# Output projection by seven block products instead of eight block multiplications, w_out split beside the last two branches

## The reference, cut to what matters

```
proj   = x @ W_in                              # 1024 x 9224, columns shared among the branches
y_i    = branch_i(proj) @ P_i                  # four branches A, B, C, M
merged = sum_i sigmoid(g_i) * y_i
out    = merged @ W_out                        # 1024 x 1024 times 1024 x 1024
x      = LayerNorm(alpha * x + out) * ln_g + ln_b
```

## Time and profile before

| | us |
|---|---|
| median of 3 runs | 1212.56 (1212.28 to 1212.91) |
| the profiled execution, whole | 1211.9 |
| its span in the profile | 1210.1 |
| mean granted clock of TensorE | 0.999 of full |
| TensorE busy | 1199.3 (99%) |
| DVE busy | 790.7 (65%) |
| POOL busy | 710.7 (59%) |
| ScalarE busy | 544.6 (45%) |
| output projection, first to last matmul | 1116.2 to 1203.6 |

### The profile page before, as it was taken

One profiled execution on the slowest core, in us unless ns is written; L12 is line 12 of the kernel. 1 busy time (PEld: TensorE's weight loads), 2 busy tenths in 40 slices (PEclk: granted clock), 3 DMA queues, 4 the chain that ended last, 5 costly groups with the idle time before them and its releaser, 6 DMA issues.

```text
span 1210.1 us, 15914 instructions
## 1 busy us (share of the span) xinstructions
PE 1199.3 (99%) x5772; PEld 1003.7 (83%) x5772; DVE 790.7 (65%) x1288; ACT 544.6 (45%) x997; POOL 710.7 (59%) x555
## 2 busy tenths in 40 slices
PE   9999999999999999999999999999999999999997
PEld 7888888888888888888888888888888888888886
DVE  5623865677576674428897666666667686877855
ACT  5433424344443444547474565656556444315000
POOL 6777887887777777878446445455533225558000
PEclk9999999999999999999999999999999999999999
DMA  8012131242323323233512111111002533377231
GB/s 280 15 55 70 35 105 35 70 140 101 108 105 105 131 92 126 105 106 118 196 48 60 36 53 53 36 53 52 20 18 101 187 115 113 105 250 253 79 123 69
DMA packets 91277, 118.61 MB, mean 98 GB/s; under 512 B 6072, under 2 KB 72632, under 8 KB 91200
## 3 DMA queue, kind: packets, MB, share of 16 engines
q1 hardware_dynamic: 90912, 117.34, 29.4%
q10 hardware_dynamic: 288, 0.26, 0.1%
HBM read 92.39 MB, written 25.20 MB: 97 GB/s over the span
## 4 chain that ended last, share of the span: by engine, by line
PE 91%; DVE 5%; ACT 2%; issue 1%; POOL 1%; DVEq 0%; ACTq 0%
PE pj L770 11%; PE pj L772 11%; PE pj L771 11%; PE pj L846 5%; PE pj L847 5%; PE pj L848 5%; PE pj L1119 4%; PE pt L770 3%; PE pt L772 3%; PE pt L771 3%; PE po L960 3%; PE pj L863 2%; PE pj L864 2%; PE pj L865 2%; PE pt L1119 2%; PE po L1119 2%
## 5 line engine op out<-in xcount | busy, mean ns | idle before, releaser
L1634 POOL TENSOR_TENSOR ring_lo<-w_pair,ring_hi 128x512 fp32r<-128x512 f32 x168 | 232.8, 1388 | 109.8 <-ACT ring_hi L1177 109.7
L1687 POOL TENSOR_TENSOR w_lo<-w_raw,w_hi 128x128 fp32r<-128x128 f32 (+1 forms) x104 | 113.0, 1105 | 131.4 <-ACT w_hi L1267 129.3
L1177 ACT ACTIVATE ring_hi<-w_pair 128x512 fp32r<-128x512 f32 x168 | 105.1, 628 | 160.4 <-PE pj L772 108.6
L1856 DVE SCALAR_TENSOR_TENSOR po<-glu,cwa,po 128x512 f32<-128x512 f32 x232 | 159.4, 747 | 20.6 <-ACT po L1228 20.6
L770 PE MATMUL pj<-t_hi,ring_hi 128*128 128x512 f32 x392 | 152.9, 390 | 0.3 <-DVE slot L1820 0.3
L771 PE MATMUL pj<-t_lo,ring_hi 128*128 128x512 f32 x392 | 152.5, 389 | 0.0
L772 PE MATMUL pj<-t_hi,ring_lo 128*128 128x512 f32 x392 | 152.5, 389 | 0.0
L846 PE MATMUL pj<-xT_hi,w_hi 128*128 128x512 f32 x320 | 126.2, 395 | 0.0
L847 PE MATMUL pj<-xT_lo,w_hi 128*128 128x512 f32 x320 | 125.3, 392 | 0.0
L848 PE MATMUL pj<-xT_hi,w_lo 128*128 128x512 f32 x320 | 125.2, 391 | 0.0
L1735 POOL TENSOR_SCALAR probs<-probs,rinv 128x128 f32<-128x128 f32 (+3 forms) x32 | 57.9, 1811 | 108.1 <-DVE rinv L2178 108.1
(11 more groups left out here) (394 smaller groups left out, 3001.9 us busy)
## 6 DMA issues: line engine op xcount, KB each, us to landing
w_pair<-in_w_in SPq DMA_DIRECT2D x28, 1024.0 KB, 5.2
gate_scratch<-slot SPq DMA_DIRECT2D x16, 1024.0 KB, 4.0
gate<-gate_scratch SPq DMA_DIRECT2D x32, 512.0 KB, 3.7
w_raw<-in_w_in SPq DMA_DIRECT2D x20, 512.0 KB, 3.9
z_scratch<-slot SPq DMA_DIRECT2D x8, 512.0 KB, 2.9
bias<-cum_scratch SPq DMA_DIRECT2D x8, 512.0 KB, 3.7
wout_raw<-in_w_out SPq DMA_DIRECT2D x8, 512.0 KB, 6.2
x_tok<-in_x SPq DMA_DIRECT2D x8, 512.0 KB, 4.3
```

The lines of the kernel that those rows point to most:

```text
L1177: nc.scalar.activation(ring_hi[:, j % RING, :, :], w_src(u, p), ACT.Copy).then_inc(s_rhi, 1)
L1634: nc.gpsimd.tensor_tensor(ring_lo[:, j % RING, :, :], w_src(u, p), ring_hi[:, j % RING, :, :], ALU.subtract).then_inc(s_rlo, 1)
L1687: nc.gpsimd.tensor_tensor(w_lo[:, j % 2, k, :], w_raw[:, j % 2, k, :], w_hi[:, j % 2, k, :], ALU.subtract).then_inc(s_wlo, 1)
L1856: nc.vector.scalar_tensor_tensor(out=acc if n < PAD_A else src, in0=src, scalar=cwa[:, ct, n:n + 1], in1=acc, op0=ALU.mult, op1=ALU.add).t ...
```

## The change

The output projection is written like the input projection: 2x2 blocks, seven products. With merged (tokens) in four pairs u of two token tiles and w_out in blocks of 512 x 512 (B11, B12, B21, B22):

- Seven w_out blocks of 512 x 512 take the place of eight rows (`out_block_hi`, `out_block_copy`, `out_block_lo`; the numbers n of `OUT_B`). Three are loaded from w_out itself (n = 0, 3, 5: B11, B21, B22), four are sums of blocks. DVE makes these sums in pairs 3 and 4 of the input projection (`block_sum`, 16 subtractions of 128 x 512, 8 in each pair, ahead of that pair's results), from rows loaded into two buffers, and SP stores them to a DRAM scratch `t_dram`, 1 MB for each row block k. The rows for pair 4 are loaded when pair 3's sums are stored. Two waits on that store are added (ScalarE before the tanh of pair 6, DVE before the sums of the layer norm).
- Pair 4 has 4 convolution steps instead of 8, pair 5 has 12 instead of 8.
- Each block, 1 MB, is loaded behind the gate load at s = M1, M3, M5, C2, C3, C5, C6; at C2 SP first waits until M5 is added up, at C6 until TensorE has finished M7. ScalarE makes the hi part (128 x 2048) and copies the scaled block to PSUM banks 4 to 7 (4 x 512), and DVE subtracts from there.
- From C2 on TensorE uses four banks for the branches and runs four halves ahead, and the last two tiles are done first halves first. DVE adds up the last two tiles itself.
- DVE (u = 0) and POOL (u > 0, and the fourth sum of u = 0) make four sums of merged blocks per u; ScalarE and POOL make hi and lo of the blocks in a ring of five. For u = 0 TensorE waits for the rests of blocks 0 to 5, before its seventh product for those of block 6.
- Results: ScalarE copies products 1, 5 and 6, DVE adds them to alpha * x (`with_copy`), then products 2, 7, 3 are added and 4 directly (`out_result`), each with its statistics. The norm of tile 6 stands before the last result. The last part is 512 columns wide.
- The gates of M2 to M5 move from 16 to 28 KB to 0 to 12 KB, other buffers move too.

```diff
-        count = (8, 8, 8, 8, 8, 8, 6, 6, 16, 16, 14, 14, 16, 16, 14, 14, 16, 16, 14, 14)[u - 4]
+        count = (4, 12, 8, 8, 8, 8, 6, 6, 16, 16, 14, 14, 16, 16, 14, 14, 16, 16, 14, 14)[u - 4]
...
+    OSEQ = [(u, p) for u in range(OU) for p in ORDER]
+    OUT_B = {1: 0, 5: 1, 6: 2, 2: 3, 7: 4, 3: 5, 4: 6}
+    LAST_C = S_END - 2
...
+                if u == 3 or u == 4:
+                    sp.wait_ge(s_ot, 8 * (u - 2))
+                    for k in range(2 * u - 6, 2 * u - 4):
+                        sp.dma_start(t_dram[k, :, :, :], ob_rows[k % 2][:, :, :].rearrange("p a (b c) -> p (a b) c", b=2)
+                                     ).then_inc(s_ots, 16)
+                if u == 2 or u == 3:
+                    if u == 2:
+                        sp.wait_ge(s_grp, 8)
+                        sp.wait_ge(s_xbl, 12)
+                    else:
+                        sp.wait_ge(s_ots, 32)
+                    for k in range(2 * u - 4, 2 * u - 2):
+                        for n in range(2):
+                            sp.dma_start(ob_rows[k % 2][:, n, :], w_out[(k + KH * n) * P:(k + KH * n + 1) * P, :]
+                                         ).then_inc(s_wor, 16)
...
-                if s == S_OF[BR_C, 2]:
+                if s == S_OF[BR_M, 1]:
                     sp.wait_ge(s_tlo, TB_PAIR * CT + 2 * NT)
                     sp.wait_ge(s_pv, PV_PAIR * CT + 2 * NT)
                     sp.wait_ge(s_zpre, CT + MP)
-                    for k in range(2):
-                        sp.dma_start(wout_raw[k][:, :], w_out[k * P:(k + 1) * P, :]).then_inc(s_wo[k], 16)
...
+                    load_out_block(0)
+                if s in (S_OF[BR_M, 3], S_OF[BR_M, 5]):
+                    load_out_block((s - S_OF[BR_M, 1]) // 2)
+                if s == S_OF[BR_C, 2]:
+                    sp.wait_ge(*added(S_OF[BR_M, 5]))
+                    load_out_block(3)
+                if s in (S_OF[BR_C, 3], S_OF[BR_C, 5]):
+                    load_out_block(4 + (s - S_OF[BR_C, 3]) // 2)
+                if s == S_OF[BR_C, 6]:
+                    sp.wait_ge(s_pj, 2 * S_OF[BR_M, DT - 1] + 2)
+                    load_out_block(6)
...
+            for h in range(2):
+                for s in range(LAST_C, S_END):
+                    pe.wait_ge(s_pjfree, half_no(s, h) - 4)
+                    p_steps(s, h, 0, CT, branch_bank(s, h))
...
+                pe.wait_ge(s_orl, j + 1)
+                if u == 0:
+                    pe.wait_ge(s_obl, KH * (7 if p == 4 else 6))
+                dst = out_bank(u, p)
+                for k in range(KH):
+                    w_h, w_l = o_ring_hi[j % O_RING][:, k, :], o_ring_lo[j % O_RING][:, k, :]
+                    hi, lo = ob_hi[OUT_B[p]][:, k, :], ob_lo[OUT_B[p]][:, k, :]
+                    nc.tensor.matmul(dst, w_h, hi, start=k == 0 and p in (1, 2, 5), stop=False, skip_group_check=True)
+                    nc.tensor.matmul(dst, w_h, lo, start=False, stop=False, skip_group_check=True)
+                    mm = nc.tensor.matmul(dst, w_l, hi, start=False, stop=k == KH - 1, skip_group_check=True)
...
+            def block_sum(k, n):
+                b11, b12, b21, b22 = (ob_rows[k % 2][:, q // 2, q % 2 * HALF:(q % 2 + 1) * HALF] for q in range(4))
+                if n == 0:
+                    dve.wait_ge(s_wor, 64 * (k // 2 + 1))
+                else:
+                    dve.wait_ge(s_ot, 4 * k + n)
+                dst, in0, in1 = ((b11, b12, b11), (b12, b22, b12), (b22, b22, b11), (b21, b21, b22))[n]
+                nc.vector.tensor_tensor(dst, in0, in1, ALU.subtract).then_inc(s_ot, 1)
...
+                    if u in (3, 4) and i < 3:
+                        for n in range(3 * i, min(3 * i + 3, 8)):
+                            block_sum(2 * (u - 3) + n // 4, n % 4)
...
+                if s >= S_OF[BR_C, 2] - 1:
+                    out_block_lo(s - S_OF[BR_C, 2] + 1)
+            for h in range(2):
+                for s in range(LAST_C, S_END):
+                    p_half(s, h, branch_bank(s, h))
+                if h == 0:
+                    for n in (1, 3, 2):
+                        merged_sum(dve, nc.vector, 0, n)
+                    out_block_lo(5)
```

More of the change, by code:

```diff
@@ L1094, in _ @@
                     mscores(w + 2)
[L1095 removed]
+            for s in range(S_P + IN_M, LAST_C):
                 for h in range(2):
@@ L1149, in w_src @@
+            for j in range(NOQ):
+                out_product(j)
         def w_src(u, p):
@@ new lines, in out_block_copy @@
+            def out_block_copy(n):
+                for k in range(KH):
+                    if n == 0:
+                        act.wait_ge(s_pjfree, HALF_0 + 16)
+                    elif n < 6:
+                        act.wait_ge(s_obl, KH * (n - 1) + k + 1)
+                    elif k < 2:
+                        act.wait_ge(s_pjfree, 2 * S_END)
+                    else:
+                        act.wait_ge(s_obl, KH * n + k - 1)
+                    nc.scalar.activation(block_bank(n, k), ob_raw[n][:, k, :], ACT.Copy, scale=0.5).then_inc(s_obc, 1)
@@ L1626, in _ @@
                                      bias=eps[:, 0:1]).then_inc(s_osd, 1)
+            for s in range(S_P + IN_M + 2, S_END):
+                split_w(s // 2, s % 2, p_k(s))
+                if s in (S_OF[BR_M, 5], S_OF[BR_M, 7]):
+                    out_block_hi((s - S_OF[BR_M, 5]) // 2)
+                n = s - S_OF[BR_C, 2]
+                if n in (0, 2, 3, 4, 5):
+                    out_block_copy(max(n - 1, 0))
+                if n in (1, 2, 3, 5):
+                    out_block_hi({1: 2, 2: 3, 3: 4, 5: 5}[n])
+            for j in range(O_RING):
+                out_ring_hi(j)
+                if j == 0:
+                    out_block_copy(5)
+            out_block_hi(6)
+            for u in range(OU):
+                for p in ORDER:
+                    if p in (1, 5, 6):
+                        out_copy(u, p)
+                    if u and p == 5:
+                        out_std(2 * u - 1)
+                    if OSLOT[u, p] + O_RING < NOQ:
+                        out_ring_hi(OSLOT[u, p] + O_RING)
+                    if (u, p) == (0, 5):
+                        out_block_copy(6)
+                    if p == 4:
+                        out_std(2 * u)
+            out_std(NT - 1)
         @block.gpsimd
@@ L1778, in _, with out_lo @@
                     add_back(s - 2)
+            def out_lo(j):
+                pool.wait_ge(s_orh, j + 1)
+                nc.gpsimd.tensor_tensor(o_ring_lo[j % O_RING][:, :, :], out_src(*OSEQ[j]), o_ring_hi[j % O_RING][:, :, :],
+                                        ALU.subtract).then_inc(s_orl, 1)
+            for u in range(OU):
+                for p in ORDER:
+                    if p == 1 and u:
+                        merged_sum(pool, nc.gpsimd, u, 1)
+                        merged_sum(pool, nc.gpsimd, u, 3)
+                    out_lo(OSLOT[u, p])
+                    if p == 1 and u:
+                        merged_sum(pool, nc.gpsimd, u, 2)
+                    if p == 2:
+                        merged_sum(pool, nc.gpsimd, u, 4)
         @block.vector
@@ L2416, in _ @@
                                                    in1=lnb_b[:, part], op0=ALU.mult, op1=ALU.add).then_inc(s_yo, 1)
+            for u in range(OU):
+                for p in (1, 5, 6):
+                    if (u, p) == (0, 6):
+                        out_block_lo(6)
+                    with_copy(u, p)
+                for p in (2, 7, 3):
+                    out_result(u, p)
+                out_mean(2 * u)
+                if u < OU - 1:
+                    out_norm(2 * u)
+                    out_result(u, 4)
+                    out_mean(2 * u + 1)
+                    out_norm(2 * u + 1)
+            out_norm(NT - 2)
+            out_result(OU - 1, 4)
+            out_mean(NT - 1)
+            out_norm(NT - 1)
 def kernel(**inputs):
```

327 lines of the change are left out of this document (194 added, 133 removed).

## The result

| | before | after |
|---|---|---|
| median | 1212.49 us (4 runs) | 1227.75 us (4 runs, 1226.31 to 1228.40) |
| profiled execution, whole | 1211.9 | 1228.39 |
| its span | 1210.1 | 1226.6 |
| first matmul of the output projection | 1116.19 | 1138.02 |
| end of its last matmul | 1203.6 | 1217.7 |

The ratio is 1.0125, 95% interval 1.011 to 1.014: the change makes the kernel 15.3 us slower, and 1226 had been forecast. The sum was nearly right, but two of its terms were wrong in opposite directions.

What follows compares the result with a forecast made beforehand. TensorE, busy 99% of the span, was taken as the bound, with each wait put before it. Span 1210.1 - 10.9 + 7.0 + 13.4 + 2.3 + 1.5 = 1223.4; with 2.5 more, 1226 us, range 1211 to 1234.

Steps and rivals of the forecast that it cites:

- TensorE's work: Output projection: 336 matmuls of 512 columns instead of 384, 48 saved at 0.2267 us each, -10.9 us.
- rival D: Output projection: DVE becomes the bound through waits for POOL, 22 us per pair, +9, 1235 us; chance 0.05.
- The block sums beside pair 4: Input projection: late rows and turns with POOL delay DVE's sums and results, so TensorE waits; +7.0 us, bounds 4 and 9.
- Rivals A and C: First: pair 4 not held up, 1218 us, chance 0.12; second: one queue's transfers overlap fully, 1206 us, 0.11.
- The split of w_out: Branches M and C: larger block loads delay weights, gates and the projection's first product; +13.4 us, bounds 2 and 18.
- step (a): Branch M: blocks 1 and 2 queue ahead of weights, landing 3.1 us later each; M5's addition ends 1087.5, not 1083.0.
- rival B: Branches M and C: weights and gates pass the blocks in the queue, delays shrink to 1.5 us, 1213 us; chance 0.12.
- Step (b): Branches M to C: SP waits for M5's addition before block 3, so M7's gate lands 7.6 us later, at 1095.2.
- Step (c): Before the projection: from 1095.2 DVE has 28.4 us of work plus 6 us of late gates; first product at 1129.6.
- Clock: TensorE after two long waits: half clock until it recovers, as long as the fall; +1.5 us, between 0 and 2.9.
- End: After the last matmul: tile 6's norm makes the last result 1.8 us late, its 512 width adds 0.5; +2.3 us.

Runs made afterwards that it cites:

- e1: Changed kernel with the second eight block sums in pair 5 instead of pair 4, convolution steps 8 and 8; 1217.28 us, ratio 1.0042 to the kernel before.
- e6: Changed kernel with no rows loaded for pair 4, whose sums reuse pair 3's rows (other values); 1216.44 us, ratio 1.0036 to the kernel before.
- e7: Changed kernel with w_out blocks 1 and 2 loaded from ScalarE's DMA queue instead of SP's; 1228.30 us, ratio 1.0128 to the kernel before.
- e2: Changed kernel with SP's wait for M5's addition and block 3's load moved behind C3's weights and M7's gate; 1224.74 us, ratio 1.0101 to the kernel before.
- e4: Changed kernel with the projection's first pair in PSUM banks 0, 2, 3, each product awaiting only its own block's rests; 1219.86 us, ratio 1.0062 to before.
- e10: Changed kernel with the edits of e1, e2 and e4, block 1 loaded one tile earlier, and tile 6 stored without its norm; 1207.66 us.
- e9: Changed kernel with the edits of e1 and e4 together; 1210.72 us, ratio 0.9988 to the kernel before.

## Why the prediction was right or wrong

**TensorE's work**, -10.9: right. 336 matmuls at 0.2267 us, with two gaps of 0.24 us among them, apart from those at half clock; rival D (DVE as the bound of the projection) did not come.

**The block sums beside pair 4**, +7.0: right in mechanism and size (7.3). Its steps: rows forecast at 95.5, landed at 97.87; the store took 10.1 us and not 8. The eight sums were to end at 112.0, with two results; it was 112.3, because the turns cost less than the 16.5 us counted (a sum and its turn took about 1.7 us and not 1.9). So two errors of 2 us cancelled, which was luck. The 104.08 of the forecast is the start of DVE's next result; the seventh product itself began at 103.88. That the sums wait for POOL in turns is borne out: six of them take 9.25 us where each alone takes 0.7. Rivals A and C fall with the wait itself; e1 and e6 show its cause.

**The split of w_out**, +13.4: wrong by 3.8 us (9.6 measured), and in its step (a) wrong in mechanism. "A later small load lands behind a block" is true of the trace, but e7 shows that a queue of its own does not free the small load: 7.9 us for M4's weights there, 6.9 in the changed kernel. The forecast had ruled on rival B by that row ("against it: 1086.53"), and the row cannot tell the order of a queue from full engines. For the time here it made no difference; it would have led one to the wrong cure. Step (b) held to a microsecond: M5 added at 1097.50 (forecast 1087.5 + 10.65 = 1098.2), M7's gate at 1104.9 (1105.9). Step (c) held as a length (33.1 us from there to the first product, 34.4 forecast), but not as a cause: with M7's gate 4.4 us earlier, e2's first product came only 1.5 earlier. "DVE from 1095.2 has 28.4 us" read like a chain without slack, and the slack is in its waits for later gates, 4.9 us in the changed kernel. Inside M and C TensorE lost 4.6 us, with 7.5 forecast, and 5.0 in front, with 6. That the last was for block 5 was right (e4). That C has four PSUM banks and not eight, which the forecast named beside the late gates for the waits in C (0.5 and 1.8 us, both for a gate step), was tested by no run.

**Clock**, +1.5 with bounds 0 and 2.9: wrong, 6.6 measured, and this is the term that brings the total above the forecast. Two steps failed. The forecast took the time back at full clock from the time of the fall (half of 2.9 us, twice); the clock fell 4.9 and 4.3 us after the last matmul, not 3, and came back 4.4 and 6.1 us after the first one. And it counted two waits, while one of 2.1 us in M also had a stretch at 1.2 GHz behind it. "No row shows TensorE coming back" held for the rows it had read, but the trace before has one at its beginning: from 1.43 us on the matmuls start 0.427 us apart until 5.01, and 0.227 apart soon behind it, 3.6 us (6.1 in the changed kernel, until 7.55). With that, 2.9 us would not have stood as the upper bound. The Trainium skill ("TensorE: Matmul & The Clock Gate", Part 1) says that the array is throttled by default and that activity releases it; the traces agree, with a granted clock of 0.50 behind both waits and 1.00 from 116.7 and 1144.2 on. The measured 6.6 lies beyond the upper end that the forecast took from it.

**End**, +2.3: right (2.4), and e10 splits it: about 1.5 us for the norm of tile 6, 0.8 for the rest, which by the forecast is the width (1.8 and 0.5 forecast) and was not run by itself.

**The whole.** The forecast of the span was 1223.4, and 1226.6 was measured: 3.8 us too much for the split, 5.1 too little for the clock, 1.2 for a late start that this execution happened to have, and 0.7 of small ones. That 1226 came so near to 1227.75 is in part luck: errors of 4 and 5 us cancelled, which a sum of six terms should not be expected to do again.

## What to carry to other kernels

A saving on the bounding engine is worth what its inputs allow: 10.9 us of matmuls were saved and more than twice as much was lost in three places, to a load that waited for a store, to transfers in a stretch that was already full, and to one product that waited for six blocks because it shared their banks. Look at each new wait of the bounding engine for what it truly needs; moving eight sums by one pair and the results of the first pair to other banks gave back 17 us (e9). And count an idle stretch of TensorE at more than its length: here waits of 7.3 and 5.0 us cost another 2.1 and 2.9 us at half clock.

## What the runs showed of the hardware that was not expected

- The granted clock of TensorE returned only after 4.4 us of matmuls (pair 4) and 6.1 us (the front of the projection) in the profiled execution. In e2 and e7 the loss behind the first product was 1.9 and 2.8 us in place of 2.9, behind waits of 5.7 and 4.2 us; in e4 the same wait of 7.3 us in pair 4 cost 2.8 us in place of 2.1. So the price is not the same from run to run.
- Nor does a short wait tell by its length whether the clock falls. Behind waits of 2.1, 2.0, 2.2 and 3.1 us for M4's weights it fell (changed kernel, e2, e9, e7), behind 2.5, 2.0 and 2.0 us for the same weights it did not (e1, e4, e6).
- The first matmuls of the kernel reach full speed at different times: the same beginning put the first pair's first matmul between 5.73 and 6.72 us.
- Stores and row loads were slower than in the earlier trace rows: median 7.1 us for 1 MB of sums and 6.5 for 0.5 MB of rows, where two and four were issued one behind the other.
- A second DMA queue did not make small loads earlier while the 16 engines were busy: 7.9 us for 128 KB in e7, and for 2 us of it only the other queue's packets ran.
